# Two transformer blocks on one core: the borders of a network's stages, reordered

## What is computed

```python
def modulate(x, g, shift, scale):
    return rmsnorm(x, g) * (1 + scale) + shift
def swiglu(u, wg, wu, wd):
    return (jax.nn.silu(u @ wg) * (u @ wu)) @ wd
x = x + 0.5 * m[:, 2] * swiglu(modulate(x, norm_g[i, 0], m[:, 0], m[:, 1]), ffn_w_gate[i, 0], ffn_w_up[i, 0], ffn_w_down[i, 0])
```

## Time and profile before

| | |
|---|---|
| median of 3 runs | 2441.91 us (2436.55 to 2448.71) |
| the profiled execution, its own time | 2439.9 us |
| its span, first to last instruction | 2438.2 us |
| PE busy | 2252.1 us (92%) |
| DVE busy | 1350.0 us (55%) |
| ACT busy | 987.9 us (41%) |
| POOL busy | 182.7 us (7%) |
| mean granted TensorE clock | 0.93 of full speed |
| read from HBM | 381.06 MB, 157 GB/s over the span |

### The profile page before, as it was taken

How to read it: one execution, slowest core, us unless ns; L and a number is a source line. 1 busy time by engine, 2 the same in 40 slices (tenths; PEclk the granted TensorE clock), 3 DMA queues, 4 the chain that set the end, 5 groups by cost and what they waited for, 6 DMA issues and landing times.

```text
span 2438.2 us, 40673 instructions
## 1 busy us (share of the span) xinstructions
PE 2252.1 (92%) x17541; PEld 2114.5 (87%) x17541; DVE 1350.0 (55%) x1632; ACT 987.9 (41%) x1109; POOL 182.7 (7%) x153
## 2 busy tenths in 40 slices
PE   3899999989988899998999899989999889899987
PEld 2799899989968898998999799979999588899967
DVE  2544454459779955445444644447754444774443
ACT  2433354433324543334343533444443335444332
POOL 1000000000010000000000000003210000330000
PEclk7999999999998899999999999999997799899778
DMA  9477767743223337775555255534333033433201
GB/s 316 144 264 263 244 209 259 262 146 99 87 87 104 122 129 255 260 262 198 190 189 176 98 179 189 172 104 154 112 116 104 18 121 121 139 123 113 95 18 52
DMA packets 270791, 383.82 MB, mean 157 GB/s; under 512 B 8442, under 2 KB 230728, under 8 KB 270680
## 3 DMA queue, kind: packets, MB, share of 16 engines
q1 hardware_dynamic: 246983, 293.59, 36.8%
q0 software_dynamic: 22288, 85.02, 10.4%
q10 hardware_dynamic: 1408, 3.59, 0.4%
HBM read 381.06 MB, written 1.11 MB: 157 GB/s over the span
## 4 chain that ended last, share of the span: by engine, by line
PE 79%; DVE 13%; ACT 3%; issue 2%; DMA 2%; POOL 0%; ACTq 0%; DVEq 0%; SPq 0%
PE bank L609 22%; PE bank L610 21%; PE bank L611 21%; PE bank L631 3%; PE bank L983 2%; DVE w_lo L1625 2%; PE bank L622 2%; ACT w_hi L1201 1%; PE bank L639 1%; DVE e_long L1926 1%; DVE e_long L1944 1%; DVE rstd L1635 1%; DMA raw<-in_ffn_w_up 1%; DVE conv_acc L1875 1%; PE bank L1030 1%
## 5 line engine op out<-in xcount | busy, mean ns | idle before, releaser
L1625 DVE TENSOR_TENSOR w_lo<-raw,w_hi 128x2048 fp32r<-128x2048 f32 (+1 forms) x281 | 642.1, 2287 | 518.1 <-ACT w_hi L1201 517.8
L609 PE MATMUL bank<-u_hi,w_hi 128*128 128x256 f32 x2376 | 693.8, 292 | 26.4 <-DVE u_lo L1656 24.1
L610 PE MATMUL bank<-u_lo,w_hi 128*128 128x256 f32 x2376 | 681.8, 287 | 0.0
L611 PE MATMUL bank<-u_hi,w_lo 128*128 128x256 f32 x2376 | 681.1, 287 | 0.0
L1201 ACT ACTIVATE w_hi<-raw 128x2048 fp32r<-128x2048 f32 (+1 forms) x281 | 531.0, 1891 | 310.2 <-PE bank L611 288.5
L609 PEld LDWEIGHTS bank<-u_hi,w_hi 128*128 128x128 f32 x2376 | 464.4, 195 | 43.5 <-issue 35.0
L610 PEld LDWEIGHTS bank<-u_lo,w_hi 128*128 128x128 f32 x2376 | 466.2, 196 | 0.5 <-issue 0.5
L611 PEld LDWEIGHTS bank<-u_hi,w_lo 128*128 128x128 f32 x2376 | 465.7, 196 | 0.0
L609 PE MATMUL bank<-h_hi,w_hi 128*128 128x256 f32 x880 | 252.1, 287 | 11.6 <-DVE h_lo L1689 11.6
L610 PE MATMUL bank<-h_lo,w_hi 128*128 128x256 f32 x880 | 248.2, 282 | 0.0
L611 PE MATMUL bank<-h_hi,w_lo 128*128 128x256 f32 x880 | 248.1, 282 | 0.0
(11 more groups left out here) (334 smaller groups left out, 3621.8 us busy)
## 6 DMA issues: line engine op xcount, KB each, us to landing
ada<-in_ada_w POOLq DMA_DIRECT2D x72, 1024.0 KB, 8.3
raw<-in_w_in SPq DMA_DIRECT2D x60, 1024.0 KB, 5.1
raw<-in_ffn_w_gate SPq DMA_DIRECT2D x55, 1024.0 KB, 6.3
raw<-in_ffn_w_up SPq DMA_DIRECT2D x55, 1024.0 KB, 5.2
raw<-in_ffn_w_down SPq DMA_DIRECT2D x55, 1024.0 KB, 5.0
raw<-in_ssd_w_in SPq DMA_DIRECT2D x20, 1024.0 KB, 5.2
raw<-in_w_out SPq DMA_DIRECT2D x16, 1024.0 KB, 4.9
raw<-in_ssd_w_out SPq DMA_DIRECT2D x8, 1024.0 KB, 5.0
```

Source lines behind the costliest of these rows:

```text
L609: pe.matmul(out_, wh, xh, start=start, stop=False, skip_group_check=True)
L610: pe.matmul(out_, wh, xl, start=False, stop=False, skip_group_check=True)
L611: return pe.matmul(out_, wl, xh, start=False, stop=stop, skip_group_check=True)
L1625: ve.tensor_tensor(wlo[slot][:, 0:n], raw[slot][:, 0:n], whi[slot][:, 0:n].bitcast(F32), ALU.subtract)\
```

## The change

Three things, at the borders between stages.

1. **The last up chunk and the last down chunk of each network in halves.** `last_up` puts the chunk's two halves (24 products each) in bank 1 and bank 2 and raises `up_half` after the first. DVE and ACT make `h` in two halves, each with the four steps multiply, round, subtract on 128x256, before the two `lo_at` of the next stage as before. `last_down` does all products with the first half of `h` (after `h_half`), then all with the second (after `h_done`); the banks are released in the second pass, after every two output blocks. The last pair is taken out of PE's loop for this.
2. **`first_pair` for the first two chunks** of each network and of each projection. First the hi-by-hi and lo-by-hi products of both chunks, which read only `u_hi` (PE waits for `u_hi_done` of block k in the first half of the first chunk), then the hi-by-lo products of both. `chunk_used` of the first chunk is raised after 80 of the 96 products, that of the second after 96. In `ffn(1)` the norm `ctx_ssd` on PE stands behind the pair of chunks now, directly before the wait for its root; the programs of DVE and ACT for that norm are not changed.
3. **`keep_warm`**: 8 matmuls with no use (ones by a slice of `cols`, into a bank that is overwritten afterwards) between the norm and the first pair, in `ffn(2)`, `ffn(3)`, `ffn(4)` and in both projections.

```diff
+            def keep_warm(bk, count):
+
+                for n in range(count):
+                    pe.matmul(bank[bk][:, 0:T], ones[:, :], cols[:, 0:T], start=True, stop=True)
...
+            def first_pair(c, bk, uh, ul, u_from):
+
+                for n in range(2):
+                    take(c + n)
+                    wh, wl = chunk(c + n, KB, 256)
+                    for blk in range(2):
+                        f = slice(blk * P, (blk + 1) * P)
+                        o = bank[bk + n][:, blk * T:(blk + 1) * T]
+                        for k in range(KB):
+                            if n == 0 and blk == 0:
+                                pe.wait_ge(S["u_hi_done"], u_from + k + 1)
+                            pe.matmul(o, wh[:, k, f], uh[:, k, :], start=blk == 0 and k == 0, stop=False,
+                                      skip_group_check=True)
+                            pe.matmul(o, wl[:, k, f], uh[:, k, :], start=False, stop=False, skip_group_check=True)
+                for n in range(2):
+                    wh, _wl = chunk(c + n, KB, 256)
+                    for blk in range(2):
+                        f = slice(blk * P, (blk + 1) * P)
+                        o = bank[bk + n][:, blk * T:(blk + 1) * T]
+                        for k in range(KB):
+                            if n == 0 and blk == 0:
+                                pe.wait_ge(S["u_done"], u_from + k + 1)
+                            m = pe.matmul(o, wh[:, k, f], ul[:, k, :], start=False, stop=k == KB - 1,
+                                          skip_group_check=True)
+                    m.then_inc(S["chunk_used"], 1)
...
+                def last_up(c):
+
+                    take(c)
+                    wh, wl = chunk(c, KB, 256)
+                    for blk in range(2):
+                        f = slice(blk * P, (blk + 1) * P)
+                        for k in range(KB):
+                            m = mm3(bank[1 + blk][:, 0:T], wh[:, k, f], wl[:, k, f], uh[:, k, :], ul[:, k, :],
+                                    k == 0, k == KB - 1)
+                        m.then_inc(S[("up_half", "chunk_used")[blk]], 1)
+
+                def last_down(c):
+
+                    take(c)
+                    wh, wl = chunk(c, 2, D)
+                    for kk in range(2):
+                        if kk == 0:
+                            pe.wait_ge(S["h_half"], i + 1)
+                        else:
+                            pe.wait_ge(S["h_done"], pairs + FP)
+                        for b in range(KB):
+                            f = slice(b * P, (b + 1) * P)
+                            m = mm3(bank[4 + b // 2][:, (b % 2) * T:(b % 2 + 1) * T], wh[:, kk, f], wl[:, kk, f],
+                                    h_hi[:, kk, :], h_lo[:, kk, :], False, kk == 1)
+                            if kk == 1 and b in (1, 3, 5):
+                                m.then_inc(S["y_done"], 1)
+                    m.then_inc(S["chunk_used"], 1)
...
+                    if last:
+                        last_up(g + 3 * FP - 2)
+                    else:
+                        hidden(g + 4, 1, j - 1)
...
                 pe.wait_ge(S["x_done"], XD[["load", "ffn0", "ssd_out", "ffn2", "pool"][i]])
                 if pairs:
                     pe.wait_ge(S["silu_done"], pairs)
-                hidden(g, 0, 8 * NSP[["ctx_f0", "lat_f0", "lat_f1", "l1_f0", "l1_f1"][i]])
+                    pe.wait_ge(S["mult_done"], pairs)
+                if i > 1:
+                    keep_warm(0, 8)
+                first_pair(g, 0, uh, ul, 8 * NSP[["ctx_f0", "lat_f0", "lat_f1", "l1_f0", "l1_f1"][i]])
                 if beside:
                     beside()
-                if pairs:
-                    pe.wait_ge(S["mult_done"], pairs)
-                hidden(g + 1, 1)
                 if i == 1:
                     pe.wait_ge(S["root_done"], N["ctx_ssd"] + 1)
                 for j0, j1, ada_too in ADA_LOOPS[i]:
                     if j0 == 1:
                         pair(1, True, ada_too)
-                    with pe.Fori(max(j0, 2), j1) as j:
+                    with pe.Fori(max(j0, 2), min(j1, FP - 1)) as j:
                         pair(j, False, ada_too)
-                pe.wait_ge(S["h_done"], pairs + FP)
-                down(g + 3 * FP - 1, False, True)
+                pair(FP - 1, False, ADA_LOOPS[i][-1][2], True)
+                last_down(g + 3 * FP - 1)
...
                 norm(f"pre{l}")
                 g = G[f"proj{l}"]
                 kept = NP_ * l
+                keep_warm(4, 8)
                 for i, (_c, n, tok) in enumerate(PROJ):
                     if i >= 3:
                         pe.wait_ge(S["proj_kept"], kept + i - 2)
-                    if tok:
-                        m = project_tokens(g + i, 4 + i % 3, n)
-                    else:
-                        m = project(g + i, 4 + i % 3, u_hi, u_lo, None if i else 8 * NSP[f"pre{l}"])
-                    m.then_inc(S["chunk_used"], 1)
+                    if i == 0:
+                        first_pair(g, 4, u_hi, u_lo, 8 * NSP[f"pre{l}"])
+                    elif tok:
+                        project_tokens(g + i, 4 + i % 3, n).then_inc(S["chunk_used"], 1)
+                    elif i > 1:
+                        project(g + i, 4 + i % 3, u_hi, u_lo).then_inc(S["chunk_used"], 1)
...
-                h_rounded(FP)
+                act.wait_ge(S["mult_half"], i + 1)
+                nc.scalar.activation(h_hi[:, 0, :], hf[:, 0:T], ACT.Copy).then_inc(S["h_hi_half"], 1)
+                act.wait_ge(S["mult_done"], pairs + FP)
+                nc.scalar.activation(h_hi[:, 1, :], hf[:, T:2 * T], ACT.Copy).then_inc(S["h_hi_done"], 1)
                 hi_at(g + 3 * FP)
                 hi_at(g + 3 * FP + 1)
...
                 lo_at(g + 3 * FP - 1)
-                mult(FP)
+                ve.wait_ge(S["silu_done"], pairs + FP)
+                ve.wait_ge(S["up_half"], i + 1)
+                ve.tensor_tensor(hf[:, 0:T], hs[:, 0:T], bank[1][:, 0:T], ALU.mult).then_inc(S["mult_half"], 1)
+                ve.wait_ge(S["h_hi_half"], i + 1)
+                ve.tensor_tensor(h_lo[:, 0, :], hf[:, 0:T], h_hi[:, 0, :].bitcast(F32), ALU.subtract)\
+                    .then_inc(S["h_half"], 1)
+                ve.wait_ge(S["chunk_used"], g + 3 * FP - 1)
+                ve.tensor_tensor(hf[:, T:2 * T], hs[:, T:2 * T], bank[2][:, 0:T], ALU.mult).then_inc(S["mult_done"], 1)
+                ve.wait_ge(S["h_hi_done"], pairs + FP)
+                ve.tensor_tensor(h_lo[:, 1, :], hf[:, T:2 * T], h_hi[:, 1, :].bitcast(F32), ALU.subtract)\
+                    .then_inc(S["h_done"], 1)
                 lo_at(g + 3 * FP)
                 lo_at(g + 3 * FP + 1)
```

More of the change, by code:

```diff
@@ L649, in project @@
                     for k in range(KB):
-                        if u_from is not None and blk == 0:
-                            pe.wait_ge(S["u_done"], u_from + k + 1)
                         m = mm3(bank[bk][:, blk * T:(blk + 1) * T], wh[:, k, f], wl[:, k, f], uh[:, k, :], ul[:, k, :],
@@ L693, in down, with pair @@
                             m = mm3(bank[4 + b // 2][:, (b % 2) * T:(b % 2 + 1) * T], wh[:, kk, f], wl[:, kk, f],
-                                    h_hi[:, kk, :], h_lo[:, kk, :], opens and kk == 0 and b % 2 == 0,
-                                    closes and kk == 1)
-                        if closes and b in (1, 3, 5):
-                            m.then_inc(S["y_done"], 1)
+                                    h_hi[:, kk, :], h_lo[:, kk, :], opens and kk == 0 and b % 2 == 0, False)
                     m.then_inc(S["chunk_used"], 1)
-                def pair(j, opens, ada_too):
+                def pair(j, opens, ada_too, last=False):
                     pe.wait_ge(S["silu_done"], pairs + j)
-                    hidden(g + 2, 0, None, j - 1)
+                    hidden(g + 2, 0, j - 1)
                     if ada_too:
```

10 lines of the change are left out of this document (5 added, 5 removed).

## The result

The changed kernel is slower. Its median is 2461.38 us (2460.32 to 2468.13, 6 runs), against 2441.55 us (2436.55 to 2448.71, 6 runs) of the kernel before on the same chip; the ratio is 1.0091, with a 95% interval of 1.0068 to 1.0114, that is 17 to 28 us. The forecast was 2454, its range 2441 to 2465. The profiled execution took 2460.32 us, 20.4 more than that of before.

What follows compares the result with a forecast made beforehand. PE, with 79% of the last-ending chain, was taken as the bound. Terms -1.2 - 2.3 + 5.0 + 1.5 + 0 + 5.0 + 4.6 + 0.9 = +13.5 us on 2439.9 gave 2453.4, 2455.4 on the median's footing, stated as 2454, range 2441 to 2465.

Steps and rivals of the forecast that it cites:

- Point 1: Halves at the ends before the norms of ffn(2), (3), (4): DVE's queue allows only -0.4 us each, -1.2 together.
- Rival B: Network ends: halves pay in full, 2.24 instead of 0.4 us at four ends, giving 2437.5 us; chance 0.12.
- Point 2: Halves at the end of ffn(1), where PE decided: the next norm starts at 527.0 instead of 529.3, -2.3 us.
- Point 3: Norm moved inside ffn(1): DVE's in-order queue makes the first down chunk later, +5.0 us; PE waits 5.3 for h_lo.
- the clock in `ffn(1)`: Two new long gaps of PE in ffn(1), each followed by dense products at clock 0.50: 2.3 us each, +4.6.
- Point 4: Hi first at five borders: more products left behind the last u_hi, +0.3 us each, +1.5 together.
- Point 5: Eight spare matmuls behind the norm take 1.8 us, 3.6 at half clock, in a 3.5 us gap: nothing to +0.1.
- Point 6: Clock falls in the sparse stretch at five borders, returning only with dense products: +1.0 us each, +5.0 together.
- +0.3 at each of three gathered gaps: Low clock behind gaps of about 2.5 us before the norms of ffn(3), pooling and the last norm: +0.9 together.
- Rival A: Whole kernel: the clock is neutral, so only points 1 to 4 count, +3.0 us, 2445; chance 0.23.
- Rival C: Clock losses at upper bounds: +3.4 us at five borders, 3.4 twice, 1.7 three times; 2474, half way 2466; chance 0.10.

Runs made afterwards that it cites:

- halves_only: The kernel before with only the last up and down chunk of each network in halves: 2435.38 us, ratio 1.0002.
- lo_split: The kernel before with only DVE's second w_lo at a network's end moved behind the updates of x, no halves: 2431.45 us, ratio 0.9977.
- halves_lo_split: The kernel before with the halves, and DVE's second w_lo at a network's end moved behind the updates of x: 2427.01 us, ratio 0.9940.
- norm_moved: The kernel before with only PE's norm inside ffn(1) moved behind the second chunk: 2447.63 us, ratio 1.0039.
- norm_back: The changed kernel with ffn(1) opened as before, its norm back between the first two chunks: 2453.84 us, ratio 1.0062 against the kernel before.
- fill_one: The kernel before with hi products first at five borders, eight spare matmuls behind each norm, one more for each piece: 2443.87 us, ratio 1.0020.
- warm_only: The kernel before with only the eight spare matmuls behind the norms at the five borders: 2437.77 us, ratio 0.9996.
- pair_warm_fill: The kernel before with hi products first at five borders, eight spare matmuls behind each norm, two more for each piece: 2454.67 us, ratio 1.0060.
- pair_five: The kernel before with only the hi products first in the opening pairs at the five borders: 2453.07 us, ratio 1.0059.

## Why the prediction was right, point by point

The sum was +13.5 us on the profiled execution and +20.4 were measured. The range held the median, near its upper end. The direction and the mechanism, clock losses and DVE's queue in `ffn(1)`, are those of the forecast; the size was a third too small, and the chances had put a result that cannot be told from no change (0.58) ahead of a slower one (0.38). That the number still lies in the range is helped by misses of both signs: the opening of `ffn(1)` and the mixer behind it came 2.9 us cheaper than the sum had them, the borders, the norms and the second block 9.8 us dearer. Its terms:

- **Point 1, halves at `ffn(2)` to `ffn(4)`, -1.2.** Right in size and reason: -0.48 us by the measure at each of these three ends in `halves_only`, DVE's queue deciding. That `lo_split` and `halves_lo_split` change this as they do confirms what stood behind it. Rival B, halves that pay in full, falls with `halves_only` (1.0002).
- **Point 2, -2.3 at the end of `ffn(1)`.** Measured -2.3 (from +7.6 behind the opening to +5.3 at the next norm).
- **Point 3 and the clock in `ffn(1)`, +5.0 and +4.6.** The down chunk starts 6.07 later and ends 7.6 later, against 9.6 in the sum, whose take for the two long gaps was too high. The wait was foreseen to 0.1 us (5.3, measured 5.17), the reciprocal came 1.1 us later than the 317.6 named, since the low clock on the pair delays it (two terms that the sum kept apart). `norm_moved` shows the queue alone, +5.5, and 2.0 more at the lower clock behind it; `norm_back` shows that some 7 us go with it.
- **Point 4, +0.3 for each border.** `fill_one`, at full clock and without its last spare matmul, shows 0.3.
- **Point 5, spare matmuls at nothing.** The result was right and the step wrong: 8 of them are 16 instructions and take 3.62 us. The row of the norm, x16 in the earlier trace rows, is 8 matmuls too, one for each block, and not the 16 that the text ahead of the prediction took; the sum divided by 16 and then counted 8. Instead of 1.6 us of idle time, 0.03 us are left at most in the changed kernel, and 0.55 in `warm_only`. The first product was not held up in the changed kernel (0.14 us behind the first `u_hi`). The same slip made `pair_warm_fill` too thick.
- **Point 6, +1.0 for each of five borders.** With point 4 the sum had 6.5, 7.8 were measured. The mechanism is the one named: the clock falls in the sparse stretch and comes back only with dense products; `fill_one` holds it at 1.00 and gets most back. The Trainium skill, "TensorE: Matmul & The Clock Gate", section "A second HAM failure mode: psum-queue depth-cycling", tells of a kernel that goes round through its PSUM banks, in which frequent short idling between groups of matmuls makes the clock swing between its two levels. This case's trace agrees in kind, though not with banks as the reason: pauses of 0.29 us between pairs of products, and 3.4 us or more at 0.50 that begin late in that stretch or at its end and reach over dense products, at all five borders.
- **The mis-sized term: +0.3 at each of three gathered gaps, -0.3 with point 1.** The three stretches from a pair to the next pair lost 3.6 us. The norms in front of `ffn(3)`, the pooling and the projection ran at 0.50 behind gaps of 2.71 us (5.41 instead of 3.72, as the earlier trace rows has it): 1.7 each, the bound, and not 0.3; 5.1 in all, less the 1.4 of point 1. In `norm_back` the three norms ran at 0.50 as well, in `halves_only`, with the same gap of 2.71 in front of each, none did, so the size depends on more than the gap. What decides it was not tried.
- **Missing: +4.6 in the second block.** Between the two projections the changed kernel and `norm_back` both took 398.7 and 398.8 us, the kernel before 394.7; the other kernels, with the same products there beside the opening pairs, took 390.7 (`lo_split`) to 396.2 (`pair_warm_fill`). The rows above say how it was lost: the same products at a lower granted clock, 0.88 against 0.90 (0.91 in `lo_split`). The sum had the clock at the edits alone. Why it was lower between them stays open. Without this the sum would have been 2.3 us short.

Rival A (a neutral clock) falls with `pair_five` against `fill_one`. Rival C (the upper bounds) would have needed 3.4 at each border; 1.6 came with both points 4 and 6, though its bound of 1.7 held for the three norms. The single parts add up, well within their intervals: 0.0002, 0.0039, 0.0059 and -0.0004 make 0.0096, against the measured 0.0091.

Two figures at the rivals do not follow from what stands beside them. Half way from the forecast's 2455.4 to C's 2474 is 2464.7 and not 2466. And spare matmuls worth 0.2 at each of five borders would take A's 2445 to 2444, not to the 2437.5 of B; the 0.2 itself was right, as `warm_only` shortens the five pairs by 1.3 us, 0.26 each.

## What to carry to other kernels

Before a wait is taken away, measure from the last common event to the next one that everybody waits for, on each engine: here PE's 2.24 us wait and DVE's second `w_lo` were two limits in a row. The cure of the first alone brought nothing, that of the second alone some 6 us, both together some 15. When the operands of the first products arrive slowly, do not give PE less to do for each piece but more (all products that a piece allows), and fill only the idle time ahead of dense work; and when an engine's program moves a step, move it in every other engine's program too, or its queue holds up what was ahead.

## What was not expected of the hardware

- A matmul of plain f32 operands shows as two instructions and takes 0.45 us for 128x128 by 256 columns at full clock (eight in 3.62), against 0.12 for one of the rounded (fp32r) operands: as a filler it is nearly four times as long as what it stands in for.
- Two products for each 0.79 us, behind a stretch at full clock, were followed by 0.50 at all five borders of the changed kernel; three for each 0.79 us (`warm_only`) at none.
- The same idle time of 2.71 us in front of the same three norms went with 3.4 us at 0.50 on each of them in two kernels (the changed one and `norm_back`) and on none of them in a third (`halves_only`).
- Stretches that no edit touched took 390.7 to 398.8 us, longer where the mean granted clock was lower (0.91 to 0.88): in the profile of one execution a few us between two kernels can be that alone. `halves_only` is 11.7 us faster than the kernel before in its profiled execution and level with it in the ratio.
